# Three of a mixer's four adaLN groups moved to other units, beside products of the same tile shape

## The chip, the cores and the metric

One core of one Trainium2 chip runs the whole program. The metric is device microseconds of one execution. The engines are named as the profile names them: PE is TensorE (PEld its weight loads), DVE is VectorE, ACT is ScalarE, POOL is GpSimd, SP is SyncE.

## What is computed

Two layers of a hybrid decoder trunk, for a prompt of 256 tokens and 8 samples of one token, so that the moving operand of nearly every product has 264 columns:

```python
mod = c @ w_ada[l] + b_ada[l]                    # 9 rows of 1024 for each layer
h = ada_norm(x, norm_gain[l, 0], shift, scale);  x = x + 0.5 * gate * swiglu(h, w_ffn_in[l, 0], w_ffn_out[l, 0])
h = ada_norm(x, norm_gain[l, 1], shift, scale);  x = x + gate * mixer_block(h, ...)
h = ada_norm(x, norm_gain[l, 2], shift, scale);  x = x + 0.5 * gate * swiglu(h, w_ffn_in[l, 1], w_ffn_out[l, 1])
```

The mixer projects h to three branches: a gated recurrence A (4 heads, 128 wide), a convolution with a linear recurrence B, and a gated recurrence C (4 heads, 64 wide). The branches are merged by sigmoid gates and projected once more. The products c @ w_ada are small on one side (9 rows of c, padded to 32) and long on the other (1024 rows by 9216 columns of weights for each layer).

## The kernel before, in words

**Units.** The program is a sequence of units, each one 512 KB piece of weights: 44 units for a first FFN product, 24 for the second, and 82 for the mixer, all of it twice per layer but for the mixer. `MIX` lists what each mixer unit is: 0 to 3 f, 4 to 7 bx, 8 to 11 i, 12 to 15 q, 16 and 17 cq, 18 and 19 ck, 20 bg0, 21 the small product wa, 22 to 24 bg, 25 wx, 26 to 29 cv, 30 to 33 cg, and so on. A full unit is 24 products (8 pieces of the contraction, three products each in `mm3`, lines 513 to 515: high by high, high by low, low by high).

**How a unit's weights get to PE.** SP loads them into one of RAW = 6 buffers of the tile `raw`. ACT copies them to `whi` in `split_hi` (line 470), DVE writes the remainder to `wlo` in `split_lo` (line 478), and PE waits for that in `unit_ready`. In iteration u of the mixer's loop both ACT and DVE begin with the split of unit u + LOOK, LOOK = 3, and only then do what belongs to unit u: the evacuation of its bank and the steps of the recurrences. Each engine works through its own list in order.

**The order of loads.** `LOADS` is one list for the whole program. It holds the mixer's adaLN tiles too ("a", 4 for each group, 512 KB each, also in `raw`); `load_order` puts a group's four tiles behind the load of unit place + LOOK. Load number c of the list takes buffer c % 6, and `load` (line 438) has SP wait until the load six places ahead of it in the list has been used: a unit's by DVE's split (`lo_done`), an adaLN tile by PE's products (`ada_used`). SP works through the list in order.

**adaLN groups.** `ADA_FIRST` says at which unit `ada_units` runs how many adaLN tiles. In the mixer there are four groups of 4 tiles (`MIX_ADA`), blocks 6 and 7 of the layer; a tile is 4 products of shape 128x32 (line 704). Block 6 ends with the second group: DVE turns it in `ada_ends` two iterations later. PE waits for each tile with `has_landed`.

**Other products between units.** At `AT["ca"]` = 9 PE runs `ca_sums` (line 869, shape 128x32). The recurrences' scores come in nine levels (`level`; small ones at line 920, shape 128x32 in branch A and 64x32 in C) at the units `PE_LV` = A (17, 20, 24, 28, 31, 33, ...), C (24, 28, 33, ...); level li of A waits for DVE's update of level li, the last part of which line 2153 issues one unit ahead. `sample_o` (line 995, shape 128x32) runs at 24, 28, 38 and so on between the levels of A and C.

Of the kernel before, what the change touches and what calls it, by code (L numbers as in the profile page):

```python
# [51 lines left out]
    return l * UNITS + BASE[stage] + k  # L52


MIX_ADA = (10, 16, 29, 71)
ADA_BLOCKS = [(0, 1), (0, 0)]
ADA_FIRST = {}
RING = 8
# [3 lines left out]
def plan_ada():  # L62

    for l in range(NL):
        for f, places, blocks in (
                (0, (("in0", 16), ("in0", 28), ("in0", 41), ("out0", 11)), [(l, 2), (l, 3), (l, 4), (l, 5)]),
                (1, (("in1", 18), ("in1", 36), ("out1", 11)), [(l, 8), (l + 1, 0), (l + 1, 1)])):
            if f:
                for n, place in enumerate(MIX_ADA):
                    ADA_FIRST[(l, "mix", place)] = (8 * len(ADA_BLOCKS) + 4 * n, 4)  # L70
# [183 lines left out]
def trunk(nc, x_prompt, x_sample, c_prompt, c_sample, state_hgrn, state_conv, state_rglru, state_gla,  # L254
# [4 lines left out]
    with ctx:  # L259
# [159 lines left out]
        def wait(eng, name, L, i=0):  # L419

            eng.wait_ge(S[name], L * PER[name] + i + 1)
# [99 lines left out]
        def evacuated(eng, L, what, j):  # L521

            group_done(eng, L, "mix", GI[(what, j)])
# [147 lines left out]
        def _(pe):  # L671
# [11 lines left out]
            def ada_units(n0, count):  # L683

                for n in range(n0, n0 + count):
                    b, kt = n // 8, n % 8
                    ps = ada_bank(b)
                    if kt == 0 and ADA_BEFORE[b] is not None:
                        wait(pe, "ada_turned", 0, ADA_BEFORE[b])
                    if n == FIRST:  # L690
                        pe.wait_ge(set_dve, BIAS_T)
                    if n < FIRST:
                        pe.wait_ge(first_in[FIRST_OF[n]], FIRST_COUNT[n])
                        tile = first_tile(n)
                    elif b in RING_OF:
                        if kt == 0:
                            pe.wait_ge(ring_in, 16 * RING * (RING_OF[b] + 1))
                        tile = ring[:, kt, :]
                    else:
                        has_landed(pe, "a", n)  # L700
                        tile = raw[:, raw_of("a", n), :]
                    src = tile.rearrange("p (b j i) -> p j b i", j=4, i=32)
                    for j in range(4):
                        last = mm(ps[32 * j:32 * j + 32, 0:256].rearrange("p (b i) -> p b i", i=32),  # L704
                                  cst[:, kt], src[:, j], start=(kt == 0), stop=(kt == KT - 1))
                    last.then_inc(S["ada_used"], 1)
# [17 lines left out]
            def ada_group(L, stage, k):  # L724
                if (L, stage, k) in ADA_FIRST:
                    ada_units(*ADA_FIRST[(L, stage, k)])
# [203 lines left out]
            def values_T(L, br, t, bank):  # L930

                for h in range(H):
                    last = tr(AUX[bank][:, h * P:(h + 1) * P], V[br][:, h, t * P:(t + 1) * P], ident[:, :])
                return last
# [42 lines left out]
            def sample_o(L, i, bank):  # L977
                br, j = BATCHES[i]
                wait(pe, "st_new", L, i)
                if i == 0:  # L980
                    wait(pe, "A_sc", L, 0)
                    wait(pe, "A_qs", L)
                else:
                    wait(pe, "soe", L, i - 1)
                if i == 2:
                    wait(pe, "C_vTe", L, 1)
                if i == 5:
                    wait(pe, "A_oe", L)
                if i == 4:
                    wait(pe, "C_qs", L)  # L990
                for e in range(1 if br == "A" else 2):
                    rows_ = slice(0, P) if br == "A" else slice(64 * e, 64 * e + 64)
                    q_ = qs[rows_, j if br == "A" else 4 + j]
                    for n in range(4):
                        last = mm((AUX[1], bank)[e][32 * n:32 * n + 32, 0:256].rearrange("p (b v) -> p b v", b=NB), q_,
                                  st[rows_, i % 2, :, 32 * n:32 * n + 32], start=True, stop=True)
                last.then_inc(S["so"], 1)
# [22 lines left out]
            def mixer(L):  # L1020
                g = [0]

                def take_bank():
                    if g[0] < 3:
                        group_done(pe, L, "out0", 4 + g[0])
                    if g[0] >= 3:
                        group_done(pe, L, "mix", g[0] - 3)
                    g[0] += 1
                    return BK[(g[0] - 1) % 3]


                for u, (kind, what, j) in enumerate(MIX):
# [67 lines left out]
                    for t in range(2):  # L1100
                        if u == AT["C_vT"][t]:
                            if t == 0:
                                evacuated(pe, L, "cv", 3)
                                wait(pe, "soe", L, 1)
                            else:
                                wait(pe, "C_vTe", L, 0)
                            values_T(L, "C", t, 1).then_inc(S["C_vT"], 1)
                    for br in "AC":
                        for li in range(9):
                            if u == PE_LV[br][li]:  # L1110
                                level(L, br, li)
                        for i in range(6):
                            if u == AT["so"][i] and BATCHES[i][0] == br:
                                sample_o(L, i, take_bank() if i >= 4 else None)
# [12 lines left out]
                    if u == AT["tailT"]:  # L1127
# [2 lines left out]
                        for jj in range(4):  # L1130
                            last = tr(AUX[0][0:20, jj * P:(jj + 1) * P], tail[:, jj], ident[:, :])
                        last.then_inc(S["tailT"], 1)
                    ada_group(L, "mix", u)

            ada_units(2, 5)
            for k in range(4):
# [6 lines left out]
            for L in range(NL):  # L1143
                ffn(L, 0)
                mixer(L)
                ffn(L, 1)
# [1387 lines left out]
```

## Time and profile before

| | us |
|---|---|
| median of the runs | 1433.83 (1433.67 to 1435.8, 3 runs) |
| the profiled execution | 1433.98 |
| its span, first to last instruction | 1432.2 |
| PE busy in the span | 1417.8 (99%) |
| DVE busy | 949.4 (66%) |
| ACT busy | 811.9 (57%) |
| mean DMA rate | 226 GB/s |

The span is 1.8 us shorter than the execution's own time. PE is the engine whose time counts; the mixers lie at about 241 to 490 us and 940 to 1190 us of the span. The granted clock is 0.999 of full speed over the whole of it.

### The profile page before, as it was taken

To read this page: it belongs to the slowest core of one execution; us is meant where nothing else is said; L and a number is where in the kernel's file an instruction comes from. 1 tells how busy PE (TensorE), PEld (TensorE's weight loads), DVE (VectorE), ACT (ScalarE), POOL (GpSimd) and SP (SyncE) were. 2 spreads that over 40 slices of the span, in tenths; PEclk is the share of its full clock that TensorE was granted. 3 is DMA by queue.
4 is the path that set the end of the run, shared out by engine and by line. 5 is a ranking of instruction groups with operands and counts; after the bars stand their busy time and mean duration, and the time that the engine had idled before them with its cause. 6 is when DMAs were issued, how large, how long until landed. Compare 5 with 4: busy or idle time off the path is not lost.

```text
span 1432.2 us, 33152 instructions
## 1 busy us (share of the span) xinstructions
PE 1417.8 (99%) x13908; PEld 1357.5 (95%) x13908; DVE 949.4 (66%) x1651; ACT 811.9 (57%) x1350; POOL 99.4 (7%) x154
## 2 busy tenths in 40 slices
PE   8999999999999999999999999999999999999998
PEld 6999999999999999999999999999999999999998
DVE  5764547779876797455585555587898677855553
ACT  3554435887676475444474444468876755744543
POOL 3040000011110210000000000000011002000000
PEclk9999999999999999999999999999999999999999
DMA  9998787689984669777768898676899557775661
GB/s 341 315 274 267 245 265 205 177 252 270 247 222 133 197 190 294 227 242 241 204 207 266 272 282 258 189 207 193 259 250 268 169 155 222 223 237 163 177 186 51
DMA packets 460414, 323.75 MB, mean 226 GB/s; under 512 B 11668, under 2 KB 436069, under 8 KB 460266
## 3 DMA queue, kind: packets, MB, share of 16 engines
q1 hardware_dynamic: 452240, 299.96, 71.0%
q0 software_dynamic: 7584, 20.51, 5.2%
q8 instruction: 110, 1.80, 0.5%
q10 hardware_dynamic: 442, 1.17, 0.2%
q14 instruction: 38, 0.31, 0.1%
HBM read 313.29 MB, written 8.37 MB: 225 GB/s over the span
## 4 chain that ended last, share of the span: by engine, by line
PE 89%; DVE 4%; issue 2%; ACT 2%; DMA 2%; SPq 1%; POOL 0%; DVEq 0%; ACTq 0%; POOLq 0%
PE bank L513 27%; PE bank L514 26%; PE bank L515 26%; PE bank L704 4%; DVE wlo L478 1%; DMA scale_tiles<-in_w_ada 1%; PE bank L920 1%; SPq L577 1%; PE bank L948 1%; ACT xA L1310 0%; DMA v_rows<-vrA 0%; ACT whi L470 0%; DVE x L1982 0%; DMA xA<-v_rows 0%; PE bank L743 0%
## 5 line engine op out<-in xcount | busy, mean ns | idle before, releaser
L478 DVE TENSOR_TENSOR wlo<-raw,whi 128x1024 fp32r<-128x1024 f32 (+1 forms) x432 | 512.8, 1201 | 324.5 <-ACT whi L470 323.0
L513 PE MATMUL bank<-hH,whi 128*128 128x264 f32 x2016 | 577.8, 287 | 0.0
L514 PE MATMUL bank<-hL,whi 128*128 128x264 f32 x2016 | 571.5, 283 | 0.0
L515 PE MATMUL bank<-hH,wlo 128*128 128x264 f32 x2016 | 570.9, 283 | 0.0
L470 ACT ACTIVATE whi<-raw 128x1024 fp32r<-128x1024 f32 (+1 forms) x432 | 438.2, 1033 | 173.2 <-PE bank L515 164.8
L513 PEld LDWEIGHTS bank<-hH,whi 128*128 128x128 f32 x2016 | 379.6, 188 | 11.9 <-issue 11.1
L514 PEld LDWEIGHTS bank<-hL,whi 128*128 128x128 f32 x2016 | 379.9, 188 | 0.0
L515 PEld LDWEIGHTS bank<-hH,wlo 128*128 128x128 f32 x2016 | 378.1, 188 | 0.0
L513 PE MATMUL bank<-hidH,whi 128*128 128x264 f32 x704 | 200.6, 285 | 0.0
L515 PE MATMUL bank<-hidH,wlo 128*128 128x264 f32 x704 | 200.1, 284 | 0.0
L514 PE MATMUL bank<-hidL,whi 128*128 128x264 f32 x704 | 199.5, 283 | 0.0
L1310 ACT ACTIVATE hidH<-hid 128x264 fp32r<-128x264 f32 x88 | 37.2, 424 | 171.9 <-DVE hid L1772 171.6
L513 PEld LDWEIGHTS bank<-hidH,whi 128*128 128x128 f32 x704 | 132.4, 188 | 1.3 <-issue 1.2
L515 PEld LDWEIGHTS bank<-hidH,wlo 128*128 128x128 f32 x704 | 132.7, 188 | 0.0
L514 PEld LDWEIGHTS bank<-hidL,whi 128*128 128x128 f32 x704 | 132.3, 188 | 0.0
L513 PE MATMUL bank<-eH,whi 128*128 128x266 f32 (+2 forms) x352 | 103.2, 293 | 1.1 <-DVE eL L1772 1.1
L514 PE MATMUL bank<-eL,whi 128*128 128x266 f32 (+2 forms) x352 | 101.2, 287 | 0.0
L515 PE MATMUL bank<-eH,wlo 128*128 128x266 f32 (+2 forms) x352 | 101.0, 287 | 0.0
L1310 ACT ACTIVATE sil<-bank 128x264 f32<-128x264 f32 x74 | 28.8, 389 | 89.2 <-PE bank L515 89.2
L513 PE MATMUL bank<-yH,whi 128*128 128x264 f32 x256 | 73.8, 288 | 0.0
L515 PE MATMUL bank<-yH,wlo 128*128 128x264 f32 x256 | 72.7, 284 | 0.0
L514 PE MATMUL bank<-yL,whi 128*128 128x264 f32 x256 | 72.6, 283 | 0.0
(372 smaller groups left out, 1715.3 us busy)
## 6 DMA issues: line engine op xcount, KB each, us to landing
raw<-in_w_ffn_in SPq DMA_DIRECT2D x172, 512.0 KB, 4.8
raw<-in_w_in SPq DMA_DIRECT2D x120, 512.0 KB, 5.3
ring<-in_w_ada SPq DMA_DIRECT2D x96, 512.0 KB, 6.7
raw<-in_w_ffn_out SPq DMA_DIRECT2D x64, 512.0 KB, 5.0
raw<-in_w_ada SPq DMA_DIRECT2D x32, 512.0 KB, 4.2
raw<-in_w_ffn_out SPq DMA_DIRECT2D x32, 384.0 KB, 4.6
raw<-in_w_out SPq DMA_DIRECT2D x16, 512.0 KB, 6.4
out<-st POOLq DMA_DIRECT2D x12, 512.0 KB, 7.3
```

Source lines behind the costliest of these rows:

```text
L470: nc.scalar.activation(whi[:, s, 0:w], raw_unit(n)[:, 0:w], ACT.Copy).then_inc(hi_done, 1)
L478: nc.vector.tensor_tensor(wlo[:, s, 0:w], raw_unit(n)[:, 0:w], whi[:, s, 0:w].bitcast(F), ALU.subtract).then_inc(lo_done, 1)
L513: nc.tensor.matmul(out, a, rh, start=start, stop=False)
L514: nc.tensor.matmul(out, a, rl, start=False, stop=False)
L515: return nc.tensor.matmul(out, b, rh, start=False, stop=stop)
L577: sp.dma_start(first_tile(n), src).then_inc(first_in[FIRST_OF[n]], 16)
L704: last = mm(ps[32 * j:32 * j + 32, 0:256].rearrange("p (b i) -> p b i", i=32), cst[:, kt], src[:, j], start=(kt == 0), stop=(kt == KT - 1))
L920: last = mm(out, k_[:, r_], q_c, start=True, stop=True)
L948: mm(o, v0, sc[br][:, h, 0:T], start=True, stop=False)
L1310: return nc.scalar.activation(out, in_, func, **k)
```

## The change

In both layers the first group of adaLN tiles goes from unit 10 to unit 9, the second from 16 to 17, the third from 29 to 28; the fourth stays at 71. Within a unit the group now runs ahead of the score levels instead of at the very end. So the first stands directly behind `ca_sums`, the second directly ahead of level 0 of A, the third directly ahead of level 3 (index) of A. No instruction is added or removed. As `load_order`, `ada_done` and `ada_ends` read the same table, the loads change places too: the first group's four tiles are loaded ahead of unit 13 instead of behind it, the second's behind unit 20 instead of ahead of it, the third's ahead of unit 32 instead of behind it, and block 6 is turned in iteration 19 instead of 18.

```diff
-MIX_ADA = (10, 16, 29, 71)
+MIX_ADA = (9, 17, 28, 71)
@@ mixer(L) on PE
                             values_T(L, "C", t, 1).then_inc(S["C_vT"], 1)
+                    ada_group(L, "mix", u)
                     for br in "AC":
                         for li in range(9):
                             if u == PE_LV[br][li]:
@@
                         last.then_inc(S["tailT"], 1)
-                    ada_group(L, "mix", u)
```

## Rows read from the trace of the kernel before

**Rows 1.** Page, busy time, share of span, instructions of each engine.
```profile
PE 1417.8 (99%) x13908; PEld 1357.5 (95%) x13908; DVE 949.4 (66%) x1651; ACT 811.9 (57%) x1350; POOL 99.4 (7%) x154
```

**Rows 2.** Timeline, PE, unit 28's end: start us, duration us, engine, line, output<-input, count.
```profile
334.02 0.28 PE L514 MATMUL bank<-hL,whi 128*128 128x264 f32 x1
334.14 0.28 PE L515 MATMUL bank<-hH,wlo 128*128 128x264 f32 x1
334.35 0.74 PE L920 MATMUL bank<-qA,kA 128*32 128x16 f32 x64
334.95 0.64 PE L995 MATMUL bank<-st,qs 128*32 128x256 f32 x8
...
336.18 0.39 PE L513 MATMUL bank<-hH,whi 128*128 128x264 f32 x1
336.41 0.28 PE L514 MATMUL bank<-hL,whi 128*128 128x264 f32 x1
```

**Rows 3.** Timeline, PE, the third adaLN group of the first layer.
```profile
339.28 1.93 PE L704 MATMUL bank<-raw,cst 128*32 128x256 f32 x32
341.14 0.39 PE L513 MATMUL bank<-hH,whi 128*128 128x264 f32 x1
```

**Rows 4.** Timeline, PE, the first products of level 5, in the first and the second layer.
```profile
354.83 0.74 PE L920 MATMUL bank<-qA,kA 128*32 128x16 f32 x64 [0.51 <-DVE xA L1772]
...
1054.09 0.74 PE L920 MATMUL bank<-qA,kA 128*32 128x16 f32 x64 [0.51 <-DVE xA L1772]
```

**Rows 5.** Windows, stretch ahead of level 5: length, busy time of engines, clock, DMA.
```profile
340.20:354.60 14.40, 14.12 (x184) 13.15 (x176) 14.33 (x32) 10.91 (x19) 4.07 (x6) 1.00 1.09 287
```

**Rows 6.** Timeline, DVE: splits of units 30 and 31 (one row), of unit 32, of unit 33.
```profile
335.79 2.45 DVE L478 TENSOR_TENSOR wlo<-raw,whi 128x1024 fp32r<-128x1024 f32 x2 [1.70 <-ACT whi L470]
...
340.06 1.22 DVE L478 TENSOR_TENSOR wlo<-raw,whi 128x1024 fp32r<-128x1024 f32 x1
...
345.99 1.21 DVE L478 TENSOR_TENSOR wlo<-raw,whi 128x1024 fp32r<-128x1024 f32 x1
```

**Rows 7.** Timeline, SP's DMA issues: unit 32, the group's last two tiles, unit 33.
```profile
323.05 0.37 SPq L447 DMA_DIRECT2D raw<-in_w_in  x1
...
332.98 0.33 SPq L447 DMA_DIRECT2D raw<-in_w_ada  x1
...
337.04 0.33 SPq L447 DMA_DIRECT2D raw<-in_w_ada  x1
...
338.26 0.38 SPq L447 DMA_DIRECT2D raw<-in_w_in  x1
```

**Rows 8.** DMA, issues: KB, us to landing; those at 338.26, 341.31 and 300.87.
```profile
raw<-in_w_in SPq DMA_DIRECT2D x1, 512.0 KB, 4.4
...
raw<-in_w_in SPq DMA_DIRECT2D x1, 512.0 KB, 3.9
...
raw<-in_w_in SPq DMA_DIRECT2D x1, 512.0 KB, 4.7
```

**Rows 9.** Timeline, ACT: evacuation of unit 26, splits of units 32 and 33.
```profile
328.66 0.39 ACT L1310 ACTIVATE vC<-bank 128x264 f32<-128x264 f32 x1 [1.48 <-PE bank L515]
...
337.14 1.05 ACT L470 ACTIVATE whi<-raw 128x1024 fp32r<-128x1024 f32 x1
...
342.67 1.06 ACT L470 ACTIVATE whi<-raw 128x1024 fp32r<-128x1024 f32 x1 [0.49 <-DMA raw<-in_w_in]
```

**Rows 10.** Timeline around units 20 to 22: DVE's split of 20; ACT's split of 22, evacuations.
```profile
301.58 1.23 DVE L478 TENSOR_TENSOR wlo<-raw,whi 128x1024 fp32r<-128x1024 f32 x1 [0.18 <-ACT whi L470]
...
305.99 1.05 ACT L470 ACTIVATE whi<-raw 128x1024 fp32r<-128x1024 f32 x1
307.62 0.39 ACT L1310 ACTIVATE kC<-bank 128x264 f32<-128x264 f32 x1 [0.59 <-PE bank L515]
```

**Rows 11.** Timeline, SP's issue of unit 22's load.
```profile
300.87 0.51 SPq L447 DMA_DIRECT2D raw<-in_w_in  x1
```

**Rows 12.** Timeline, PE, inside unit 21 (wa), at its fourth bank.
```profile
312.18 0.28 PE L515 MATMUL bank<-zH,wlo 128*128 128x264 f32 x1
312.57 0.39 PE L513 MATMUL bank<-zH,whi 128*128 128x264 f32 x1
```

## The prediction

> **What bounds the kernel now.** I read the page first: PE is busy for 1417.8 of 1432.2 us [rows 1], so PE's own list sets the time, and a change can act in two ways only: by making that list shorter, or by making PE stand still. I then read PE's timeline through both mixers and looked at the distance from one start to the next. Inside a unit it is 0.12 us (334.02 to 334.14) [rows 2]. Where the tile shape changes it is longer: 0.21 us from the last 128x128 product to the first 128x32 one (334.14 to 334.35), and 0.23 us between the first two products after the way back (336.18 to 336.41) [rows 2]. These two are what the change is after. Last I looked for places at which PE waits. There is one idle entry for each layer, 0.51 us ahead of level 5 of branch A, released by DVE [rows 4], and one smaller pause in unit 21, 0.39 us between two starts (312.18 to 312.57) [rows 12]. These two places decide about the change. Ahead of the first one DVE is busy for 14.33 of 14.40 us [rows 5]: from its split of unit 32 at 340.06 [rows 6] to PE's level 5 at 354.83 [rows 4] it has no free time at all. Whatever delays that split delays PE's level by as much, and anything that PE saves in that stretch only makes its wait longer. The second layer shows the same 0.51 us at 1054.09 [rows 4], and its other rows repeat those of the first some 699 us later, so all below counts twice.
>
> **Part 1, the joined products.** A group that stands next to products of the same shape saves one way in and one way out: (0.21 - 0.12) + (0.23 - 0.12) = 0.20 us. With three groups and two layers the PE list gets 6 x 0.20 = 1.2 us shorter. That is the change's whole gain. The group's own length, 1.86 us from start to next start (339.28 to 341.14) [rows 3], stays: it moves from behind unit 10 to ahead of it, and so on. The third kind of neighbour, C's 64x32 products, is not touched.
>
> The Trainium skill, page "TensorEngine Tiling (Array Packing)", section "Key Properties", says that a change of tiling mode drains TensorE. The trace agrees for the change from 128x128 to 128x32, with the 0.09 and 0.11 us above. If that rule were all there is to this change, it would come out 1.2 us faster; that is the first rival.
>
> **Part 2, the third group's loads (unit 32).** `load` lets load c start only when load c - 6 has been used. Written out, the list before is ... 26 27 28 29 30 31 32 a a a a 33 34, and unit 32 waits for the split of unit 26. SP issues it at 323.05 [rows 7], long ahead of ACT's split of it at 337.14 [rows 9]. The list after is ... 26 27 28 29 30 31 a a a a 32 33 34. Six places ahead of unit 32 now stands unit 30. DVE splits units 30 and 31 in 2.45 us from 335.79 [rows 6], so 30 is done at about 337.0; before, the group's last tile waited for just that, and went at 337.04 [rows 7]. So unit 32 is issued at 337.04 instead of 323.05. A load of that kind lands after 3.9 us on a quiet queue and after 4.4 us with another just ahead of it [rows 8]. The queue should be quiet by then, as the group's last tile is now issued at 332.98 already, and I take 3.9: it lands at 340.94. ACT, which would have begun the split at 337.14, begins at 340.94 and ends 1.04 us later, at 342.0. DVE then splits unit 32 at 342.0 instead of 340.06 [rows 6]: 1.95 us late. As DVE has no free time up to level 5 [rows 5], the level starts 1.95 us late as well. With 4.4 us it is 2.45 us. Behind ACT's stalled split are queued the evacuation of unit 29, a table load, the square root and the split of unit 33, which began at 342.67 [rows 9]. Even if all of them came later by the full 340.94 - 337.14 = 3.8 us, unit 33's split would end at 342.67 + 3.8 + 1.06 = 347.5, and DVE, late itself, wants it at 345.99 + 1.95 = 347.9 [rows 6]; so they add nothing. PE itself meets the group's last tile early: it is issued at 332.98 and lands at 336.9 at the earliest if it takes those 3.9 us, while PE wants it at 334.35 + 3/4 x 1.86 = 335.75. PE waits some 1.1 us there, but it has about 2.5 us to wait at level 5 anyway, so this costs nothing as long as part 2 holds, and up to 1.1 us a layer less PE's old wait of 0.51 if it doesn't. The third group's own 0.20 us is lost in the same way, as it lies between the start of this chain and level 5.
>
> **Part 3, the second group's loads (unit 22).** The same count, for the group at 16: unit 22 waited for the group's first tile, which PE had used long before unit 20, and went at 300.87 right behind unit 21 [rows 11]. After, it waits for the split of unit 20, which DVE begins at 301.58 and ends at about 302.75 [rows 10], so it goes 1.88 us later. Before it took 4.7 us to land [rows 8], at 305.6, and ACT began its split at 305.99 [rows 10]. After, it lands at 306.65 with 3.9 us and at 307.45 with 4.7. ACT's split takes 1.05 us, of which the next instruction overlaps 0.1; the evacuation that follows, 307.62 before [rows 10], then starts at 307.6 to 308.4. From there ACT has no free time until it frees the fourth bank of unit 21, the 0.39 us pause [rows 12]. So PE is 0.0 to 0.8 us late there, and I take 0.4. What the first two groups saved (0.40 us) is gone too, since the ACT chain is now held by the load and not by PE. Behind that point ACT waits for PE again (1.48 us idle at 328.66) [rows 9], so the 0.4 us is handed on to the chain of part 2.
>
> **Part 4, what I cost at nothing.** Unit 13 now waits for the split of unit 11 instead of 7; by the same count it reaches ACT under 1 us late, and ACT's work of unit 10 moves by the 1.86 us by which PE ends unit 10 later. ACT and DVE both have idle time before the end of unit 15, so this is made good; if it were not, it would cost up to 1.86 us a layer less the slack. Block 6 is turned one iteration later, 0.7 us of DVE behind the remainder of the convolution, into a stretch in which DVE next waits for ACT. Units 14 to 20 and 26 are loaded earlier or as before. POOL's state loads wait for products at unit 28 that come some 2 us later, and for DVE's transposes that are late by as much as PE is.
>
> The Trainium skill, page "DMA: Bandwidth & Descriptors", section on the anatomy of one DMA, gives about 2.0 us plus bytes over 436 GB/s, an estimate of 3.2 us for 512 KB. The trace shows 3.9 to 4.7 us [rows 8]. By the page's figure part 2 would be 1.25 us and part 3 nothing, and the sum 2.5 us slower; the sum here goes by the rows.
>
> **The sum.** A layer: 0.4 (part 3, with the first two joins gone) + 1.95 (part 2, with the third join gone) = 2.35 us. Two layers: 4.7 us. Against the profiled execution's 1433.98 us that is 1438.7 us; the median of the runs lies 0.15 us lower, which gives 1438.5. Low end of this case: 0.0 and 1.95 with 0.4 us of joins still kept, 1.55 us a layer, 1436.9 us. High end: 0.8 and 2.45, 3.25 us a layer, 1440.3 us.
>
> **The rivals.**
> - The change does what its shape says, and the late load is hidden. The mechanism: DVE's chain ahead of level 5 isn't as tight as the row says, or unit 32 lands within 2 us. The point from which it decides is a landing before 339.0, that is within 2.0 us of the issue at 337.04, so that ACT's split ends by 340.06. Then the joins up to unit 17 count, and the third only adds to PE's wait: 4 x 0.20 = 0.8 us saved, or 1.2 us if that wait shrinks too: 1432.7 to 1433.0 us. For it speaks that PE's list does get shorter; against it that no load of this size in the rows lands in under 3.9 us.
> - Half of it is hidden: part 2 holds but part 3 doesn't, and DVE makes up some of the delay because the evacuations of units 30 and 31 no longer keep it waiting, 1 us a layer in all: 1435.8 us. Against it speaks the 14.33 of 14.40 us.
> - The late loads meet a crowd. With the group's tiles used early, units 33 to 36 are issued right behind unit 32, and they share its engines. If it then takes 6.5 us, as loads in a burst do, part 2 is 4.5 us and the sum 4.9 us a layer: 1443.6 us. Against it speaks that 32 is issued first and unit 33 more than 1 us later.
>
> **How the numbers follow.** About 0.2% (2.9 us) is what a measurement of this kernel can tell from no change: faster is below 1431.0, slower above 1436.7. The forecast gets 0.6, the first rival 0.15, the half-hidden case 0.12, the crowd 0.13. Of the forecast nearly all is slower, and of the crowd all, together 0.70. Within 0.2% are the first rival, the half-hidden case and a little of the forecast, 0.28. Faster by more than 0.2% would need over twice the joins' gain, 0.02. The forecast's own range is 1436.9 to 1440.3. The range that should hold 8 in 10 reaches down over the half-hidden case to the first rival's upper part and up a little beyond the forecast: 1433.0 to 1441.0.
>
> **What the profile after would show.** Part 1: 64 products of line 920 directly behind the group's line 704, with no 0.2 us between. Part 2: an idle entry of ACT at the split of unit 32 of some 3 us, released by the DMA `raw<-in_w_in`, one of DVE on ACT of about 2 us behind it, and PE's wait at level 5 grown from 0.51 to about 2.5 us, less whatever PE already waited at the group's last tile, in both layers. Part 3: the issue of unit 22 at about 302.7 and an idle entry of ACT on it; the pause in unit 21 longer. If level 5's wait stays near 0.5 us, part 2 is wrong; if it grows with ACT's split on time, the cause is another one. The prediction fails most easily on the time to landing: each 0.5 us of it is 1 us of the result.

## The result and the profile after

| | before | after |
|---|---|---|
| median of the runs beside each other, us | 1434.49 (1433.67 to 1436.61, 6 runs) | 1447.86 (1443.11 to 1452.8, 6 runs) |
| the profiled execution, us | 1433.98 | 1446.62 |
| its span, us | 1432.2 | 1444.8 |
| granted clock, mean | 0.999 | 0.995 |

The changed kernel is slower: the ratio is 1.0093, interval 1.0081 to 1.0106, some 13.4 us. The forecast was 1438.5 us with 1433.0 to 1441.0 as its range. The direction was right, the loss was nearly three times the forecast one, and the range did not hold it.

The page's first part, where [rows 1] stood before. Nothing is added to any engine:
```profile
PE 1417.4 (98%) x13908; PEld 1360.1 (94%) x13908; DVE 949.7 (66%) x1651; ACT 811.1 (56%) x1350; POOL 99.2 (7%) x154
```

The waits of PE: what it waits for, us in total, how often, the longest. Before, level 5's entry was 0.51 in each layer [rows 4], and the other three rows were not there:
```profile
PE bank L920 <- DVE xA L1772: 6.7, 2, 3.6
...
PE bank L920 <- issue: 2.9, 1, 2.9
...
PE bank L513 <- ACT tmp L1310: 1.4, 2, 0.7
PE bank L513 <- issue: 1.2, 2, 0.9
```

**Where the 12.6 us of the two spans lie.** I laid the starts of the same products side by side. Up to the first mixer PE is 0.11 us late. Behind the first join it is 0.24 us early, behind the second 0.57 us early, behind unit 21 it is 1.24 us late, at level 5 4.19 us late (359.02 against 354.83), a little further on 10.06 us. There it stays up to the second mixer. In that one 9.71 behind the first join, 10.50 behind unit 21, 12.64 at level 5 (1066.73 against 1054.09), and about that to the end. So the first layer loses 9.95 us and the second 2.55 us.

Timeline, PE, level 5 and what follows, first layer (answers to the first of [rows 4]):
```profile
359.02 1.05 PE L920 MATMUL bank<-qA,kA 128*32 128x16 f32 x64 [3.63 <-DVE xA L1772]
360.01 0.81 PE L920 MATMUL bank<-qC,kC 64*32 64x16 f32 x61
363.68 0.29 PE L920 MATMUL bank<-qC,kC 64*32 64x16 f32 x3 [2.86 <-issue]
363.90 0.59 PE L513 MATMUL bank<-hH,whi 128*128 128x264 f32 x1
364.28 0.42 PE L514 MATMUL bank<-hL,whi 128*128 128x264 f32 x1
```
The same in the second layer (answers to the second of [rows 4]):
```profile
1066.73 0.74 PE L920 MATMUL bank<-qA,kA 128*32 128x16 f32 x64 [3.08 <-DVE xA L1772]
1067.40 0.73 PE L920 MATMUL bank<-qC,kC 64*32 64x16 f32 x64
1068.06 0.39 PE L513 MATMUL bank<-hH,whi 128*128 128x264 f32 x1
1068.29 0.28 PE L514 MATMUL bank<-hL,whi 128*128 128x264 f32 x1
```
Three things are to be seen. PE's wait for DVE has grown from 0.51 to 3.63 and 3.08 us. In the first layer 64 products that take 0.74 us take 1.05, and behind them the distance between products is 0.22 us up to 368.90 where it is else 0.12. And in the first layer PE stands still once more for 2.86 us in the middle of level 2 of branch C, without waiting for another engine as far as the profile shows. The second layer has the wait alone, and so shows what the chain of late loads costs by itself.

Windows of the changed kernel: length, busy time of PE, PEld, DVE, ACT, POOL, granted clock of PE, DMA share, GB/s:
```profile
360.00:365.00 5.00, 2.14 (x77) 1.99 (x70) 4.93 (x10) 0.00 (x0) 0.89 (x1) 0.50 1.01 300
355.00:372.00 17.00, 10.51 (x180) 10.12 (x179) 12.54 (x24) 4.61 (x10) 2.06 (x3) 0.70 0.77 218
...
1060.00:1070.00 10.00, 6.92 (x175) 6.66 (x174) 9.93 (x15) 4.80 (x10) 4.79 (x7) 1.00 0.89 262
```
The granted clock is 0.50, the lower level of 1.2 GHz, from 360 to 365 us, soon behind the end of the wait of 3.63 us at 359.02. Behind the wait of 3.08 us in the second layer it is 1.00. The Trainium skill, page "TensorE: Matmul & The Clock Gate", section "Part 1: The HAM clock gate", says that the engine's clock is halved when it has been little busy; the first layer agrees with its 0.50, the second shows that a wait of this size does not always bring it about.

**The chain of late loads.** The timelines of SP, ACT and DVE, each with its own columns as in [rows 6, 7, 9, 10]: first unit 22, then unit 32, in the first layer.
```profile
302.59 0.38 SPq L447 DMA_DIRECT2D raw<-in_w_in  x1
...
307.92 1.06 ACT L470 ACTIVATE whi<-raw 128x1024 fp32r<-128x1024 f32 x1 [2.39 <-DMA raw<-in_w_in]
...
309.01 1.22 DVE L478 TENSOR_TENSOR wlo<-raw,whi 128x1024 fp32r<-128x1024 f32 x1 [2.31 <-ACT whi L470]
310.15 1.25 DVE L1772 TENSOR_TENSOR zL<-tmp,zH 128x1056 fp32r<-128x1056 f32 x1
```
```profile
338.31 0.38 SPq L447 DMA_DIRECT2D raw<-in_w_in  x1
...
343.16 1.06 ACT L470 ACTIVATE whi<-raw 128x1024 fp32r<-128x1024 f32 x1 [4.64 <-DMA raw<-in_w_in]
...
344.25 1.23 DVE L478 TENSOR_TENSOR wlo<-raw,whi 128x1024 fp32r<-128x1024 f32 x1 [2.83 <-ACT whi L470]
```
Unit 22 was issued at 302.59 instead of 300.87 [rows 11] and took 5.3 us to land. Unit 32 was issued at 338.31 instead of 323.05 [rows 7] and took 4.8 us. DVE's split of unit 32 began at 344.25 instead of 340.06 [rows 6], 4.19 us late, and level 5 is 4.19 us late as well: DVE handed on the whole of it, as [rows 5] said it would.

What PE waited for at unit 21 (answers to [rows 12]):
```profile
311.50 0.36 PE L513 MATMUL bank<-zH,whi 128*128 128x264 f32 x1 [0.91 <-issue]
...
313.81 0.39 PE L513 MATMUL bank<-zH,whi 128*128 128x264 f32 x1 [0.69 <-ACT tmp L1310]
```
The second of these is the pause of [rows 12] grown, the fourth bank that ACT frees. The first is new. The profile calls it "issue", but unit 21's products multiply `zH` and `zL`, and DVE writes `zL` at 310.15 to 311.40, directly behind its late split of unit 22. That this is what PE waited for is read from these times and from the program; no run took it apart.

### The profile page after: what moved, and what is told of

Read it like the earlier page. It is cut to its first block, busy times and chain, and to the rows that moved or that the text cites. A ratio compares the mean times of both kernels' runs of the same rounds, so it can differ in the third digit from the quotient of the medians.

```text
span 1444.8 us, 33152 instructions
## 1 busy us (share of the span) xinstructions
PE 1417.4 (98%) x13908; PEld 1360.1 (94%) x13908; DVE 949.7 (66%) x1651; ACT 811.1 (56%) x1350; POOL 99.2 (7%) x154
## 4 chain that ended last, share of the span: by engine, by line
PE 91%; DVE 4%; issue 2%; DMA 1%; ACT 1%; SPq 1%; DVEq 0%; ACTq 0%
PE bank L513 28%; PE bank L514 27%; PE bank L515 27%; PE bank L704 4%; DVE wlo L478 1%; PE bank L920 1%; DMA scale_tiles<-in_w_ada 1%; DMA raw<-in_w_in 1%; SPq L577 1%; PE bank L948 1%; DVE x L1982 0%; PE bank L995 0%; PE bank L924 0%; PE bank L743 0%; PE bank L1016 0%
```

## The experiments

All ratios are against the kernel before, run beside each kernel.

**Each group by itself.** The first group alone, at unit 9, with the group still at the end of the unit:
```diff
-MIX_ADA = (10, 16, 29, 71)
+MIX_ADA = (9, 16, 29, 71)
```


> Only the first group is moved (10 to 9, behind the gate sums), with its loads. T: unit 13 is split 0.4 us late and nobody waits for it; two joins, 0.4 us faster, 1433.7 us, hardly to be told from before. A wait on PE at unit 13 or 14 would show part 4 of the prediction wrong.

Measured: 1433.53 us (1433.11 to 1434.21, 10 runs), ratio 0.9991, 0.9982 to 1.0001. PE waits nowhere for it. Between 265 and 300 us of the first layer ACT has one new wait for a load, 0.4 us at unit 13's split (waits of ACT in that stretch); in the second layer it is 0.2 us:
```profile
ACT whi L470 <- DMA raw<-in_w_in: 0.4, 1, 0.4
```
So the early loads of the first group cost nothing, as part 4 held.

The second group alone:
```diff
-MIX_ADA = (10, 16, 29, 71)
+MIX_ADA = (10, 17, 29, 71)
@@ mixer(L) on PE
+                    ada_group(L, "mix", u)
                     for br in "AC":
...
-                    ada_group(L, "mix", u)
```


> Only the second group is moved (16 to 17), with its loads behind unit 20. T: unit 22 is issued 1.9 us later and lands 5.3 us after that, unit 21's pauses on PE grow to 1 to 2.5 us in all, the level 5 wait stays at 0.5 us: 1 to 4 us slower. R: 0.4 us faster, two joins.

Measured: 1435.71 us (1435.13 to 1437.67, 10 runs), ratio 1.0011, 1.0001 to 1.0020. PE's waits show both pauses of unit 21, the fourth bank in both layers and the one for `zL` in one:
```profile
PE bank L513 <- ACT tmp L1310: 1.4, 2, 0.7
...
PE bank L513 <- issue: 0.8, 1, 0.8
```

The third group alone, the same edit with `MIX_ADA = (10, 16, 28, 71)`.

> Only the third group is moved (29 to 28, ahead of the levels), with its loads ahead of unit 32; the first two stay. Theory T (late load of unit 32): ACT waits some 4 to 5 us for the load, PE's wait at level 5 grows from 0.5 us to 3 to 4 us in each layer, and where it does a stretch at the lower clock may follow; 5 to 12 us slower than before, the larger part of the change. Rival R (the moved products delay the recurrence): the same time, but with ACT's split of unit 32 on time. Rival S (unit 22 is the larger part): under 3 us slower.

Measured: 1441.08 us (1438.54 to 1447.52, 7 runs), ratio 1.0055, 1.0034 to 1.0077. The seven times fall in two groups: four at 1438.54 to 1441.08, three at 1446.43 to 1447.52, and the second group has the lower mean clock (0.993 to 0.995 against 0.996 to 0.999). The profiled execution, 1438.60 us, is one of the first. Its waits of PE:
```profile
PE bank L920 <- DVE xA L1772: 3.7, 2, 2.8
...
PE bank L704 <- DMA raw<-in_w_ada: 2.1, 2, 1.7
```
Level 5 waits 0.89 and 2.78 us, less than the 3 to 4 expected. PE had already stood still at the group's own last tile, 1.72 us in the first layer and 0.34 in the second. The clock stays up. So this execution lost 4.5 us against the median of the kernel before beside it, 1434.11 us, without any loss to the clock. No trace was kept of the slower three, so what came on top in them isn't shown.

**Products or loads?** A rival was that it is the group's new place on PE, in front of the levels, that costs the time, and not the order of the loads. So I left PE's order as it was before and moved the loads alone, first those of the third group:
```diff
 MIX_ADA = (10, 16, 29, 71)
+MIX_LOAD = (10, 16, 28, 71)
@@ load_order
-    groups = {unit_at(l, stage, place) + LOOK: n for (l, stage, place), (n, _) in ADA_FIRST.items() if stage == "mix"}
+    groups = {unit_at(l, stage, MIX_LOAD[MIX_ADA.index(place)]) + LOOK: n for (l, stage, place), (n, _) in ADA_FIRST.items()
+              if stage == "mix"}
```


> PE's order is that of the kernel before, only the third group's four loads go ahead of unit 32's instead of behind it. T: the products' places don't matter, the load's does: again 5 to 12 us slower, level 5's wait 3 to 4 us. R: within 0.5 us of before, as no product has moved.

Measured: 1440.61 us (1439.48 to 1441.03, 4 runs), ratio 1.0042, 1.0027 to 1.0057. No product of PE moved, and level 5 waits 2.4 us in both layers, less than expected, too (waits of PE; line 922 is line 920 of the kernel before):
```profile
PE bank L922 <- DVE xA L1774: 4.8, 2, 2.4
```
Window of the same kernel behind its first wait; the clock has fallen here too:
```profile
354.00:360.00 6.00, 3.58 (x140) 3.30 (x139) 5.96 (x11) 1.82 (x3) 0.90 (x2) 0.79 0.96 311
```
The rival is gone: with no product moved, the loads alone take 6.5 us by the medians, where the third group's whole move takes 7.0.

The second group's loads alone, `MIX_LOAD = (10, 17, 29, 71)`:

> PE's order is that of the kernel before, only the second group's four loads go behind unit 20's instead of ahead of it. T: as the run with the second group alone, 1 to 4 us slower, with the tile pair not joined. R: no difference from before.

Measured: 1436.78 us (1435.15 to 1438.15, 10 runs), ratio 1.0016, 1.0007 to 1.0025, no less than the 1.0011 with the products moved too. PE waits 0.7 us in unit 21 and 0.6 us at the group's own tile, which now lands later than PE wants it (each in one layer; lines 515 and 706 are 513 and 704 of the kernel before):
```profile
PE bank L515 <- ACT tmp L1312: 0.7, 1, 0.7
PE bank L706 <- DMA raw<-in_w_ada: 0.6, 1, 0.6
```

**What does the wait trigger?** The first layer lost 5.87 us behind level 5. If clock and pause are consequences of PE having stood still, then products that fill the wait must do away with both, although they add work. The changed kernel with eight products more, whose results nothing reads:
```diff
+                    if u == PE_LV["A"][5]:
+                        wait(pe, "C_sc", L, 1)
+                        for _ in range(8):
+                            mm(AUX[2][:, 0:256], ones[:, 0:P], ones[:, :], start=True, stop=True)
```


> The changed kernel with eight more products (128x128 on 256 columns, some 0.43 us each, 3.4 us in all, results not used) on PE ahead of level 5, where it waits 3.1 to 3.6 us. Theory C (the second half of the loss is PE's clock, which falls after the long idle time): the fill takes the place of the wait, the clock stays at its upper level through 355 to 372 us, and the pause named issue may go too: 1440 to 1442 us, 6 to 8 us less than the changed kernel, though it does more. Rival D (the time behind the wait is lost to crowded DMA, not to PE's idleness): no gain, 1447 to 1451 us, as the fill adds a little.

Measured: 1441.29 us (1440.25 to 1442.51, 4 runs), ratio 1.0045, 1.0029 to 1.0061. That is 6.6 us less than the changed kernel with more to do. Timeline, PE, of this kernel at level 5 of the first layer:
```profile
355.50 3.62 PE L1112 MATMUL bank<-ones 128*128 128x256 f32 x16
359.27 0.74 PE L920 MATMUL bank<-qA,kA 128*32 128x16 f32 x64 [0.16 <-DVE xA L1776]
359.94 0.73 PE L920 MATMUL bank<-qC,kC 64*32 64x16 f32 x64
```
and the window that answers to 355.00:372.00 above:
```profile
355.00:372.00 17.00, 16.84 (x244) 16.02 (x243) 16.93 (x36) 9.72 (x23) 2.31 (x3) 1.00 0.76 221
```
Level 5 begins no earlier (359.27 against 359.02), but the clock stays at 1.00, the level's products take 0.74 us again and the second pause is not there. What is left over the kernel before, 6.55 us, is close to the load chain's delay of the two layers, 4.08 + 2.55 = 6.63 us by the offsets above. For the clock this run settles the question. For the pause it doesn't, because the eight products also push everything behind them further along PE's instruction list, and that alone can take the pause away, as the last experiments show.

**Is it enough that DVE is late?** The kernel before, without any move, with DVE writing the remainder of unit 32 twice more:
```diff
+                    if u == 29:
+                        n_ = n_unit + LOOK
+                        dve.wait_ge(hi_done, n_ + 1)
+                        for _ in range(2):
+                            V_(tt(wlo[:, n_ % SLOTS, 0:UC], raw_unit(n_)[:, 0:UC], whi[:, n_ % SLOTS, 0:UC].bitcast(F),
+                                  ALU.subtract))
+                            own(L)
```


> The kernel before, all loads and products in their old places, but DVE writes unit 32's remainder three times instead of once (2.3 us more in iteration 29). T (only DVE's lateness ahead of level 5 counts, whatever makes it late): level 5's wait goes from 0.5 to some 2.8 us in both layers and the result is as with the third group's loads moved alone, 1439 to 1441 us. Rival L (the late load harms by itself, through crowded queues): clearly less than that, under 1439 us.

Measured: 1442.31 us (1440.58 to 1443.23, 4 runs), ratio 1.0052, 1.0034 to 1.0070. Waits of PE, and the window behind the first of the two waits:
```profile
PE bank L920 <- DVE xA L1772: 5.8, 2, 2.9
```
```profile
360.00:366.00 6.00, 6.00 (x44) 6.00 (x43) 5.91 (x12) 2.50 (x6) 0.65 (x1) 0.82 1.10 288
```
The two waits grew by 2.4 us each, 4.8 us together, and the kernel lost some 7.6 us by the medians. Its 1442.31 us lie 1.3 us above what was expected. The rest is the clock, 0.82 here and 0.72 in 1060 to 1066: in the first layer PE is 2.50 us late at level 5 (357.33 against 354.83) and 4.03 us late at line 933 behind it (363.20 against 359.17), 1.5 us more, and in the second layer 1.5 us again. There is no second pause. No load was touched: DVE's lateness is enough for the wait and for the clock.

**What are the joins worth by themselves?** Two kernels, one with the products' places of the changed kernel and one with those of the kernel before, that both leave out the loads of the first three groups; those groups' products read another tile instead. The edit, on top of either:
```diff
+NO_LOAD = {ADA_FIRST[(l, "mix", MIX_ADA[i])][0] for l in range(NL) for i in (0, 1, 2)}
@@ load_order
-        if n in groups:
+        if n in groups and groups[n] not in NO_LOAD:
@@ ada_units on PE
+                        if n - n % 4 in NO_LOAD:
+                            pe.wait_ge(set_mask, 16)
+                            tile = mask[:, :, :].rearrange("p k c -> p (k c)")
+                        else:
```


> The changed kernel, but the tiles of the first three mixer groups are not loaded: their products read another tile that stays in place (that part of the adaLN products is left out, so block 6 and half of block 7 are not computed from the weights). No unit waits for a buffer held by them. T: level 5's wait is 0.5 us or less, the clock stays up, and against its partner without loads at the old places it is faster by the joins alone, 0.8 to 1.2 us. R (the moved products harm): slower than its partner.

> The partner: the kernel before with the same three groups' tiles not loaded, products at the old places. T: as before or up to 1 us faster, 1433 to 1434.5 us; the 0.51 us at level 5 stay, since nothing there waited for a load.

Measured: 1432.91 us (1432.54 to 1434.54, 10 runs) with the joins, 1434.46 us (1434.17 to 1436.01, 10 runs) without: 1.55 us. The second kernel takes as long as the kernel before (ratio 1.0002, 0.9993 to 1.0012). Level 5's two waits (line 927 here) are 1.6 us together with the joins (first row), more than expected, and 1.0 us without (second row), so 0.6 us of what PE's list lost in length went into waiting:
```profile
PE bank L927 <- DVE xA L1779: 1.6, 2, 0.8
```
```profile
PE bank L927 <- DVE xA L1779: 1.0, 2, 0.5
```

**The joins without the late loads.** The kernel before with the first group at 9 and the second at 17 ahead of the levels, the third left at 29, and the loads of the second where they were:
```diff
-MIX_ADA = (10, 16, 29, 71)
+MIX_ADA = (9, 17, 29, 71)
+MIX_LOAD = (9, 16, 29, 71)
```
with `MIX_LOAD` used in `load_order` as above, and `ada_group` ahead of the levels.

> The joins that cost no load: first group at 9, second at 17 with its tiles loaded ahead of unit 20 as in the kernel before, third left at 29. T: unit 22 is issued at 300.4 as before, four joins save 0.8 us at most, and ACT's chain at unit 21 may keep half of it: 1433.3 to 1434.1 us. If it is slower than before by 1 us or more, the joins themselves do harm.

Measured: 1433.08 us (1432.43 to 1434.62, 10 runs), ratio 0.9988, 0.9979 to 0.9998: faster than both kernels, though against the kernel before by little more than the interval allows. At unit 21's fourth bank two starts lie 0.40 and 0.45 us apart in the two layers, about as before (0.39), unit 25 has a new pause of 0.2 us in the first layer, and level 5 waits 0.4 us.

**The second pause.** Two more executions of the changed kernel, to see whether it comes back at the same product.

> The changed kernel once more, for its second-order losses. Theory C2: the wait at level 5 (3 to 4 us a layer) and the late unit 22 are there every time; what differs is the stretch at the lower clock behind the wait, and whether a second pause of 2 to 3 us named issue falls in the middle of level 2 of C. Time within 1443 to 1453 us, higher where more of the two layers show that pause.

Measured: 1451.13 us; the pause is there in both layers (3.25 us each). Timeline, PE, first layer:
```profile
358.05 0.74 PE L920 MATMUL bank<-qA,kA 128*32 128x16 f32 x64 [3.30 <-DVE xA L1772]
358.72 0.75 PE L920 MATMUL bank<-qC,kC 64*32 64x16 f32 x61
362.72 0.29 PE L920 MATMUL bank<-qC,kC 64*32 64x16 f32 x3 [3.25 <-issue]
```


> The same again. C2: as above. If the pause named issue is gone in both looks and the time is near 1443 us, it goes with the slower executions; if the time is over 1447 us without it, its place is another one.

Measured: 1447.05 us; the pause is there in the first layer alone (waits of PE):
```profile
PE bank L920 <- DVE xA L1772: 6.3, 2, 3.3
...
PE bank L920 <- issue: 3.1, 1, 3.1
```
In the first layer it falls behind the 61st of the 64 products each time, in the second layer of 1451.13 us behind the 48th. That could be something in these products, or something in the list of PE's instructions at this place. The program begins with 38 tiny products whose results aren't used (`FILL`, line 39); more of them move everything behind them along PE's instruction list and leave the products and their data as they are.
```diff
-FILL, KEEP = 38, 4
+FILL, KEEP = 46, 4
```


> The changed kernel with eight more small products in PE's opening fill (46 instead of 38, line 678; 16 more matmul records and their weight loads), 1400 us ahead of or far from the place in question. Theory F (the pause is a late fetch of PE's instructions, which come in blocks): the block's end moves by 16 records, so in the first layer the pause, which stood after the 61st of the 64 records of level 2 of C, stands some 16 records earlier, after about the 45th, and a packet of the instruction queue lands 2 to 3 us before PE goes on. Rival G (these products or their operands stall): the pause stays after the 61st record.

Measured, one execution: 1443.13 us. Level 5 waits 3.37 and 2.80 us, and there is no second pause in either layer, though the clock has fallen in the first (the level's products take 1.06 us). Timeline, PE, first layer:
```profile
359.59 1.06 PE L920 MATMUL bank<-qA,kA 128*32 128x16 f32 x64 [3.37 <-DVE xA L1772]
360.58 0.84 PE L920 MATMUL bank<-qC,kC 64*32 64x16 f32 x64
```
Neither expectation was met: not "still behind the 61st", and not "eight products further up".

The same with `FILL` at 62:

> The same with 24 more products (62 instead of 38, 48 more records). F: the pause stands after about the 13th record of level 2 of C, or is gone if the fetch now falls into the wait ahead of level 5. G: it stays after the 61st.

Measured, one execution: 1445.18 us. No pause at that level, but two of the same kind in places that had none, where PE's list is plain unit products. First layer, between units 25 and 26 (1.92 us more at 1031.98, in the second layer):
```profile
325.13 0.29 PE L515 MATMUL bank<-zH,wlo 128*128 128x264 f32 x1
327.75 0.38 PE L513 MATMUL bank<-hH,whi 128*128 128x264 f32 x1 [2.34 <-issue]
327.93 0.42 PE L514 MATMUL bank<-hL,whi 128*128 128x264 f32 x1
```
Behind this pause the clock is at 0.50 too, for about 3 us. So the pause does not belong to these products; where it falls goes with PE's instruction list, as far as three executions without a shift and two with one can tell.

PE's wait at level 5 can have its part in the pause, but is not needed for it. In the three traces of the changed kernel the pause follows all four waits of 3.29 us and more, and neither of those of 3.08 and 3.06 us. With the list shifted by eight products it does not follow a wait of 3.37 us, and with 24 it comes where PE had not waited. The eight products that filled the wait shift what follows in the first layer by as much as the first of these shifts, so the fill can't show that the wait brings the pause.

The queue that the profile names "instruction" shows in the same sense: it moves a block now and then, and in windows of 0.5 us one can see when. At the pauses in level 2 of branch C the block before came 13.5 to 16 us earlier (345.5, then 361.0 in the changed kernel), where 5.5 to 12.5 us lie between blocks in the same stretch of the runs without that pause, and PE goes on some 2 to 3 us after a block; at 327.75 and 1031.98 too (blocks in the windows from 325.0 and 1029.5). That fits PE running out of instructions while its next block is on the way. It isn't shown: at those last two places the block before had come only 11.5 and 10 us earlier, which gaps without a pause reach as well. Why a block comes late in some executions and not in others, no run here shows.

## Why the prediction failed, step by step

Of the 12.6 us that the profiled execution lost, the sum had 4.7. Of the rest, 5.87 us lie behind level 5 of the first layer, where the sum had nothing; 1.7 us lie ahead of it in that layer (4.08 against 2.35), and 0.2 us in the second (2.55 against 2.35).

**Part 1, the joins: right in kind, too small.** The forecast was 0.20 us each, 1.2 us in all; 1.55 us was measured, after 0.6 us more of waiting, so PE's list became about 2.1 us shorter. The offsets say 0.35 us for the first join, 0.33 for the second and 0.27 to 0.31 for the third. The rows show the missing part. Timeline, PE, at `ca_sums`, of the kernel before:
```profile
270.02 1.12 PE L869 MATMUL bank<-tmp,wca 128*32 128x264 f32 x16
271.07 0.39 PE L513 MATMUL bank<-hH,whi 128*128 128x264 f32 x1
```
and of the changed kernel:
```profile
270.13 1.12 PE L869 MATMUL bank<-tmp,wca 128*32 128x264 f32 x16
271.05 1.93 PE L704 MATMUL bank<-raw,cst 128*32 128x256 f32 x32
```
The sixteen products occupy 1.05 us if a 128x128 product follows and 0.92 us if one of their own shape does. I had counted only the distance behind the first product on the way back, 0.23 against 0.12, and not these 0.13 us ahead of it. That the third join's gain would go into the wait at level 5 was right.

**Part 2, the load of unit 32: mechanism right, size too small.** The place of the issue was right: it would have been at 337.04, and went at 338.31 only because of the 1.27 us that came from unit 21. The term that was mis-sized is the time to landing: 4.8 us in the first layer and 4.2 us in the second, where I took 3.9 for a quiet queue (4.4 was the high end). That is 0.9 us more in the first layer. The 3.9 was one single load. The page of the kernel before had 5.3 us as the median of the 120 loads `raw<-in_w_in`, and unit 32's own load, issued at 323.05, had taken 6.6 us there while nothing waited for it. The estimate of 3.2 us from the Trainium skill's page "DMA: Bandwidth & Descriptors" would have been further off; the fit in its section "Anatomy of one DMA" is for transfers that GpSimd issues, and these are issued by SP. So DVE's split came 4.19 us late, 1.27 handed on and 2.92 of its own, against 1.95.

**Part 3, the load of unit 22: too small in the first layer.** I took 0.4 us for what it adds, with the first two joins gone. Against that, PE was 1.24 us late behind unit 21, 1.13 us more than ahead of the mixer. In the second layer it was 10.50 - 10.06 = 0.44 us, near the forecast. Two terms are behind the difference: the landing took 5.3 us where 4.7 was my high end; and DVE, which I had not looked at here, does its split of unit 22 before the remainder `zL` that unit 21 itself needs, so the late load stopped PE in the unit ahead of it as well (0.91 us). I had followed ACT's list behind the stalled split and not DVE's.

**The second layer is near the sum as forecast.** 2.35 us a layer was the sum; the second layer lost 2.55 us.

**The step that failed: the term that was not there.** The forecast priced PE's wait at its own length and put what follows it at nothing, without a reason. In the first layer of the profiled execution the wait of 3.63 us was followed by 5.87 us more: 2.86 us of a second pause, and about 3.0 us at the lower clock, as the products from 363.90 to 368.90 start 0.22 us apart instead of 0.12. That is the larger half of the miss. It differs between executions: those of the changed kernel lie between 1443.11 and 1452.8 us (mean clock 0.997 at the fastest, 0.993 at the slowest) where those of the kernel before lie within 3 us, and of the three that were traced the one of 1451.13 us has two pauses and those of 1446.62 and 1447.05 us have one. The lower clock is shown to be a consequence of PE's wait: it stayed at 1.00 when the wait was filled, and with two more writes of DVE it fell without a pause, for 1.5 us in each layer. In the changed kernel the pause falls into the stretch at the lower clock, so the 3.0 us need not be the wait's alone. The pause's cause stays open.

**Which waits bring the clock down stays open.** Over all runs in which level 5 waited 2 us or more, it fell behind waits of 3.63, 3.46, 3.37, 3.30, 3.29, 3.06, 2.90, 2.87, 2.69 and two of 2.4 us (eleven in all), and not behind 3.08, 2.80, 2.78 and 2.09 us. So the length of the wait alone doesn't decide.

**Part 4 was right**, as the first group's move alone shows. **The rivals:** that the late load is hidden is out, by the wait of 3.1 to 3.6 us. Half hidden is out as well. The crowd, with 6.5 us to landing, came to 1443.6 us and was nearest in time, but for a reason that the rows don't show: the landing was 4.2 to 5.3 us. The group's own last tile, for which I had PE waiting some 1.1 us, did keep it waiting where the third group was moved alone, 1.7 us in the first layer and 0.3 in the second.

## What to carry to other kernels

- A product that is moved takes its loads with it when one table orders both. In a ring of buffers, count who stands a ring's length ahead of every load in the new list; a unit's load that waited for something long done can come to wait for something that happens now. Keep a load where it was if moving it would make another one wait, and move the products alone: that gave the one version whose interval lies below the kernel before, by 0.1%.
- Follow the list of every engine that stalls behind a late split, DVE's as well as ACT's: what belongs to an earlier unit may stand behind it.
- On an engine that sets the time, a wait of some 3 us can cost more than itself. Give such a case a range upwards for the clock.
- Take a load's time from many rows, the median and the spread, and not from a single one: the forecast's 3.9 us was one load, and the median of its kind was 5.3.
- An instruction put in to test one cause also moves all behind it along the engine's list. Shift the list by as much with the cause left in, and see whether the effect stays.

## What the runs showed of the hardware

- PE's clock went to its lower level (0.50 granted) behind eleven of fifteen single waits of 2.1 to 3.6 us in the middle of a dense stretch. That cost 1.5 us each time in the kernel with two more writes of DVE. Products whose results nobody reads, put into the wait, kept it at 1.00; that kernel was 6.6 us shorter than the changed one, part of it because the second pause was gone.
- PE can stand still for 1.9 to 3.3 us with no engine to wait for. The place changed when PE's instruction list was shifted by 8 and by 24 products, one execution each.
- A group of 128x32 products between 128x128 ones cost 0.27 to 0.35 us more than one beside its own shape; at `ca_sums` 0.09 us of it lay on the way in and the rest on the way out.
- The 512 KB loads that were followed one by one took 3.9 to 6.6 us (median of 120 in the kernel before: 5.3). What sets them apart, no run here shows.
